# Delta-rule projections: conv taps out of PSUM, all weight remainders on VectorE, first weights by piece

## The reference, cut to what matters

```python
proj = x @ w_in                                   # (256, 1024) @ (1024, 4112)
qkv, z, b, a = jnp.split(proj, [3072, 4096, 4104], axis=-1)
qkv = jax.nn.silu(causal_dwconv(qkv, conv_w))     # 4 taps over time, per channel
q, k, v = jnp.split(qkv, [1024, 2048], axis=-1)   # then 8 heads of 128
q, k = l2norm(q) * 128 ** -0.5, l2norm(k)         # needs sum(t * t) over each head
beta = jax.nn.sigmoid(b)
g = -jnp.exp(a_log) * jax.nn.softplus(a + dt_bias)
... # chunked delta rule, gate with silu(z), w_out, layer norm; then SwiGLU, S5,
... # a mixture of experts, and the second block
```

## Time and profile before

| what | value |
|---|---|
| executions, device time | 1888.09 us median of 3 (1887.85 to 1892.72) |
| profiled execution, first to last instruction (span) | 1885.6 us |
| PE busy | 1613.8 us, 86% |
| DVE busy | 1103.5 us, 59% |
| ACT busy | 700.6 us, 37% |
| POOL busy | 133.3 us, 7% |
| mean granted TensorE clock | 0.914 of full speed |
| stage of the change | first matmul 14.29 us, first z matmul 118.56 us, last z matmul 142.4 us |

### The profile page before, as it was taken

How to read it: one execution, slowest core, us unless ns; L and a number is a source line. 1 busy time by engine, 2 the same in 40 slices (tenths; PEclk the granted TensorE clock), 3 DMA queues, 4 the chain that set the end, 5 groups by cost and what they waited for, 6 DMA issues and landing times.

```text
span 1885.6 us, 25406 instructions
## 1 busy us (share of the span) xinstructions
PE 1613.8 (86%) x9980; PEld 1187.4 (63%) x9980; DVE 1103.5 (59%) x1621; ACT 700.6 (37%) x920; POOL 133.3 (7%) x79
## 2 busy tenths in 40 slices
PE   5896976999774486999999999497699999999995
PEld 5896845898673365888888888386444343443434
DVE  6946646999848755888888887765321212112136
ACT  4443104444320133777677776241112121211222
POOL 5540000000015400000000000000000000000000
PEclk9888987999875596999999999798799999999998
DMA  8321013544530042888888888173299999999950
GB/s 324 135 90 46 3 45 119 192 177 160 231 112 1 0 179 84 306 326 318 305 312 328 332 316 326 40 318 129 110 408 425 422 423 426 421 424 423 423 213 23
DMA packets 36217, 442.82 MB, mean 235 GB/s; under 512 B 5296, under 2 KB 5680, under 8 KB 8624
## 3 DMA queue, kind: packets, MB, share of 16 engines
q1 hardware_dynamic: 33264, 433.58, 58.3%
q10 hardware_dynamic: 2880, 8.23, 1.2%
HBM read 440.74 MB, written 1.05 MB: 234 GB/s over the span
## 4 chain that ended last, share of the span: by engine, by line
PE 54%; DVE 6%; ACT 1%; issue 0%; DVEq 0%; ACTq 0%
PE psum L215 53%; DVE sb_split L1569 1%; ACT sb_split L1564 1%; DVE sb_work L1972 1%; DVE sb_small L290 1%; PE psum L1608 1%; PE psum L1511 0%; PE psum L1858 0%; DVE sb_ring_r L260 0%; DVE sb_xres L1808 0%; DVE sb_work L349 0%; DVEq L211 0%; PE psum L331 0%; DVE sb_work L313 0%; DVE sb_xres L310 0%
## 5 line engine op out<-in xcount | busy, mean ns | idle before, releaser
L215 PE MATMUL psum<-sb_work 64*64 64x64 f32 (+11 forms) x3472 | 444.2, 374 | 96.1 <-POOL sb_work L1428 40.3
L215 PEld LDWEIGHTS psum<-sb_work 128*64 128x64 f32 (+5 forms) x3472 | 254.3, 169 | 266.2 <-issue 187.2
L215 PE MATMUL psum<-sb_split 128*128 128x512 f32 (+1 forms) x1680 | 376.8, 383 | 8.0 <-DVE sb_split L1569 8.0
L215 PEld LDWEIGHTS psum<-sb_split 128*128 128x128 f32 x1680 | 309.7, 189 | 65.6 <-DVE sb_split L1569 11.2
L1569 DVE TENSOR_TENSOR sb_split<-sb_ring,sb_split 128x2048 fp32r<-128x2048 f32 (+1 forms) x144 | 302.5, 2111 | 75.2 <-ACT sb_split L1564 74.3
L1564 ACT ACTIVATE sb_split<-sb_ring 128x2048 fp32r<-128x2048 f32 (+1 forms) x144 | 253.8, 1774 | 116.5 <-PE psum L215 106.7
L215 PE MATMUL psum<-sb_ring,sb_work 128*64 128x512 f32 (+1 forms) x848 | 207.9, 597 | 2.9 <-ACT sb_work L1881 1.3
L215 PEld LDWEIGHTS psum<-sb_ring,sb_work 128*64 128x64 f32 (+1 forms) x848 | 69.2, 143 | 135.9 <-issue 134.8
L215 PE MATMUL psum<-sb_xT_r,sb_ring_r 128*128 128x256 f32 x512 | 146.9, 287 | 0.0
L1970 DVE TENSOR_TENSOR sb_work<-sb_work,psum 128x512 f32<-128x512 f32 x16 | 11.0, 687 | 188.2 <-ACT sb_work L1891 188.2
L1891 ACT ACT_TABLE_LOAD x16 | 20.5, 1283 | 264.2 <-PE psum L215 264.2
(11 more groups left out here) (386 smaller groups left out, 2337.3 us busy)
## 6 DMA issues: line engine op xcount, KB each, us to landing
sb_ring<-moe_wide SPq DMA_DIRECT2D x48, 2048.0 KB, 8.2
sb_ring<-moe_up SPq DMA_DIRECT2D x48, 2048.0 KB, 11.5
sb_work<-moe_down SPq DMA_DIRECT2D x32, 2048.0 KB, 10.5
sb_ring<-w_dense SPq DMA_DIRECT2D x25, 2048.0 KB, 8.0
sb_ring<-moe_last SPq DMA_DIRECT2D x24, 1536.0 KB, 6.7
sb_work<-moe_up SPq DMA_DIRECT2D x16, 2048.0 KB, 13.1
sb_ring<-ffn_wide SPq DMA_DIRECT2D x12, 2048.0 KB, 8.3
sb_ring<-ffn_last SPq DMA_DIRECT2D x6, 1536.0 KB, 6.7
```

Source lines behind the costliest of these rows:

```text
L215: return nc.tensor.matmul(o, lhsT, rhs, start=start, stop=stop, **kw)
```

## The change

- **Conv taps.** ACT no longer copies a piece into `raw`. It writes the last tap (the newest sample times its weight) straight from PSUM into `qkvT` (one ACTIVATE with a scale). DVE adds the other three taps with three scalar_tensor_tensor, each reading the PSUM bank itself, over 255, 254 and 253 columns. They are spread over laps: lap c adds tap 2 of piece c, tap 1 of piece c - 1 and tap 0 of piece c - 2. PE may reuse a bank when `conv_done` says that the last tap was added.
- **Remainders.** All 32 are on DVE, that of piece c + 3 at the head of lap c. POOL has none.
- **Squares.** They move from POOL to ACT, piece c - 3 in lap c, behind the silu of piece c - 2.
- **z.** The fourth z piece's high part (ACT) and remainder (DVE) now stand ahead of the norm's arithmetic, the last four remainders behind the gates'.
- **Loads.** The first six units are laid out piece by piece in memory (a piece is 1024 numbers in a row for each partition), and the first unit is loaded as four transfers of 512 KB, of which the first three have semaphores of their own, so that ACT can begin with the first piece alone.

```diff
@@ gdn: helpers @@
-            w = tile[:, gd_unit(s) % RING, :].rearrange("p (k n) -> p k n", k=DC)
-            return w[:, :, (s % 4) * P:(s % 4 + 1) * P] if s < QKV else ...
+            w = tile[:, gd_unit(s) % RING, (s % 4) * D:(s % 4 + 1) * D]
+            return w.rearrange("p (k n) -> p k n", k=DC if s < QKV else 2)
         def gd_high(act, s):
-            unit_ready(act, gd_unit(s))
+            if s < 3:
+                act.wait_ge(sem(f"piece_loaded{s}"), 16)
+            else:
+                unit_ready(act, gd_unit(s))
@@ gdn_tensor @@
                 if c >= 4:
-                    pe.wait_ge(sem("qkv_evac"), c - 3)
+                    pe.wait_ge(sem("conv_done"), c - 3)
...
-            pe.wait_ge(sem("qkv_evac"), QKV - 3)
+            pe.wait_ge(sem("conv_done"), QKV - 3)
...
-            pe.wait_ge(sem("qkv_evac"), QKV - 2)
+            pe.wait_ge(sem("conv_done"), QKV - 2)
@@ gdn_scalar, for c in range(QKV + 2) @@
                 if c < QKV:
                     gd_high(act, c + 3)
                     act.wait_ge(sem("qkv_ps"), c + 1)
-                    act.activation(raw[:, c, TAPS - 1:], bank[c % 4][:, 0:SEQ], ACT.Copy).then_inc(sem("qkv_evac"), 1)
+                    act.activation(qkvT[:, c, :], bank[c % 4][:, 0:SEQ], ACT.Copy, scale=conv_w[:, c, TAPS - 1:TAPS])\
+                       .then_inc(sem("tap_done"), 1)
                 if c >= 2:
                     act.wait_ge(sem("conv_done"), c - 1)
                     act.activation(qkvT[:, c - 2, :], qkvT[:, c - 2, :], ACT.Silu).then_inc(sem("silu_done"), 1)
+                if 3 <= c < 2 * HEADS + 3:
+                    act.wait_ge(sem("silu_done"), c - 2)
+                    act.activation(sq[...], qkvT[:, c - 3, :], ACT.Square).then_inc(sem("sq_done"), 1)
@@ gdn_vector @@
-            gd_low(v, 2)
-            for c in range(QKV):
-                if c + 3 < QKV and gd_on_vector(c + 3):
-                    gd_low(v, c + 3)
-                v.wait_ge(sem("qkv_evac"), c + 1)
-                ... # tensor_scalar, then three linked scalar_tensor_tensor out of raw
+            for s in range(3):
+                gd_low(v, s)
+            def tap(c, k):
+                late = TAPS - 1 - k
+                acc = qkvT[:, c, late:]
+                return v.scalar_tensor_tensor(acc, bank[c % 4][:, 0:SEQ - late], conv_w[:, c, k:k + 1], acc, ALU.mult, ALU.add)
+            for c in range(QKV + 2):
+                if c < QKV:
+                    gd_low(v, c + 3)
+                    v.wait_ge(sem("tap_done"), c + 1)
+                    tap(c, 2).then_inc(sem("tap2_done"), 1)
+                if 1 <= c <= QKV:
+                    v.wait_ge(sem("tap2_done"), c)
+                    tap(c - 1, 1).then_inc(sem("tap1_done"), 1)
+                if c >= 2:
+                    v.wait_ge(sem("tap1_done"), c - 1)
+                    tap(c - 2, 0).then_inc(sem("conv_done"), 1)
@@ gdn_gpsimd @@
-            g.memset(raw[:, :, 0:TAPS - 1], 0.0).then_inc(sem("pad_done"), 1)
-            for s in range(GD_PIECES):
-                ... # remainders and squares
@@ sync @@
-            for u in range(RING):
+            for i in range(4):
+                sp.dma_start(ring[:, 0, i * D:(i + 1) * D], I["w_dense"][DENSE_AT[U_QKV]][:, i * D:(i + 1) * D])\
+                  .then_inc(sem(f"piece_loaded{i}" if i < 3 else "unit_loaded0"), 16)
+            for u in range(1, RING):
                 dense(u, U_QKV)
```

More of the change, by code:

```diff
@@ L353, in program @@
         cw = Carver(work, 0, WORK)
-        raw = cw(QKV, SEQ + TAPS - 1)
+        cw(QKV, SEQ + TAPS - 1)
         qkvT = cw(QKV, SEQ)
@@ L430, in gd_high, with gd_low @@
             act.activation(gd_buffer(s), gd_piece(ring, s), ACT.Copy).then_inc(sem("gdn_high"), 1)
[L432 to L435, removed]
+        def gd_low(v, s):
+            v.wait_ge(sem("gdn_high"), 1 + s + 1)
+            v.tensor_tensor(gd_piece(ring_r, s), gd_piece(ring, s), gd_buffer(s).bitcast(F32), ALU.subtract)\
+             .then_inc(sem("gdn_low"), 1)
         def gd_split(pe, s):
[L439 to L443, removed]
+            pe.wait_ge(sem("gdn_low"), 1 + s + 1)
         def gdn_tensor(pe):
-            pe.wait_ge(sem("gdn_low_vector"), 1)
             for c in range(QKV):
                 if c >= 4:
-                    pe.wait_ge(sem("qkv_evac"), c - 3)
+                    pe.wait_ge(sem("conv_done"), c - 3)
                 gd_split(pe, c)
@@ L490, in gdn_tensor @@
                         ins.then_inc(sem("z_used"), 1)
-            pe.wait_ge(sem("qkv_evac"), QKV)
+            pe.wait_ge(sem("conv_done"), QKV)
             pe.wait_ge(sem("silu_done"), QKV)
@@ L660, in gdn_scalar @@
                     act.activation(qkvT[:, c - 2, :], qkvT[:, c - 2, :], ACT.Silu).then_inc(sem("silu_done"), 1)
+                if 3 <= c < 2 * HEADS + 3:
+                    act.wait_ge(sem("silu_done"), c - 2)
+                    act.activation(sq[(c - 3) // HEADS][:, (c - 3) % HEADS, :], qkvT[:, c - 3, :], ACT.Square)\
+                       .then_inc(sem("sq_done"), 1)
             act.wait_ge(sem("gates_vector"), 1)
@@ L666, in gdn_scalar @@
             act.activation(sp_a[:, :, :], sp_a[:, :, :], ACT.Ln, bias=1.0).then_inc(sem("gates_act"), 1)
+            gd_high(act, QKV + 3)
             act.wait_ge(sem("gates_vector"), 2)
             act.activation(rn[:, :, :], rn[:, :, :], ACT.Sqrt).then_inc(sem("gates_act"), 1)
-            for s in range(QKV + 3, GD_PIECES):
+            for s in range(QKV + 4, GD_PIECES):
                 gd_high(act, s)
@@ L716, in gdn_vector @@
             v.wait_ge(sem("gdn_high"), 1)
-            v.tensor_tensor(gxl[:, :, :], xT[:, :, :], gxh[:, :, :].bitcast(F32), ALU.subtract).then_inc(sem("gdn_low_vector"), 1)
-            gd_low(v, 2)
-            v.wait_ge(sem("pad_done"), 1)
-            for c in range(QKV):
-                if c + 3 < QKV and gd_on_vector(c + 3):
-                    gd_low(v, c + 3)
-                v.wait_ge(sem("qkv_evac"), c + 1)
[L724 to L730, removed]
+            v.tensor_tensor(gxl[:, :, :], xT[:, :, :], gxh[:, :, :].bitcast(F32), ALU.subtract).then_inc(sem("gdn_low"), 1)
+            for s in range(3):
[6 more added lines that the diff above has]
+                if c < QKV:
+                    gd_low(v, c + 3)
+                    v.wait_ge(sem("tap_done"), c + 1)
[6 more added lines that the diff above has]
+                    tap(c - 2, 0).then_inc(sem("conv_done"), 1)
             v.wait_ge(sem("gates_ps"), 1)
@@ L739, in gdn_vector @@
             dve_link(v, v.tensor_scalar(sp_t[:, :, :], sp_t[:, :, :], 0.0, None, ALU.max))
+            gd_low(v, QKV + 3)
             v.wait_ge(sem("gates_ps"), 2)
@@ L2684, in layouts, with by_piece @@
     glu, w2in = inp["s5_w_glu"][0], inp["w_in_2"][0]
-    units = cols(w_in, 0, 8) + cols(inp["gdn_w_out"][0], 0, 2) + cols(inp["s5_w_in"][0], 0, 2)
+    def by_piece(unit):
+        return unit.reshape(P, DC, 4, P).transpose(0, 2, 1, 3).reshape(P, UNIT)
+    units = [by_piece(u) for u in cols(w_in, 0, 6)] + cols(w_in, 6 * 512, 2) + cols(inp["gdn_w_out"][0], 0, 2) + cols(inp["s5_w_in"][0], 0, 2)
     units += cols(glu, 0) + cols(glu, D) + cols(glu, 512) + cols(glu, D + 512)
```

3 lines of the change are left out of this document (removed).

## The result

| | before | changed |
|---|---|---|
| median, us | 1890.68 (8 runs, 1887.85 to 1893.18) | 1899.04 (8 runs, 1894.04 to 1901.97) |
| ratio | | 1.0047, 95% interval 1.0035 to 1.0058 |
| profiled execution | span 1885.6 | 1898.75, span 1897.0 |
| first matmul | 14.29 | 11.46 |
| one-column matmuls begin | 106.37 | 110.81 |

Slower by 0.47%: 8.4 us between the medians of all runs; 7.6 were forecast, 1895.7 in all. The same views as in the earlier trace rows, now of the changed kernel: the head of its page and its timeline of PE.

The account below looks back on a forecast made before the run. PE was taken as the bound, waiting for remainders on a late DVE. Earlier start, turn-taking laps and slower one-column matmuls put z 7.6 us late: 1885.6 + 7.6 = 1893.2, with 2.5 around it 1895.7; range 1887 to 1905.

Parts of the forecast that it names:

- Start: Before the first matmul: with unit 0 loaded in four parts, PE starts at 11.4 instead of 14.29, 2.9 us earlier.
- Lap: Main loop: ACT and DVE take turns, 4.24 us a lap, 3.79 without the square; PE waits about 1.4.
- End of the loop: After the last lap: one-column matmuls wait for tap 0, begin at 112.7 instead of 106.37; loop 6.3 us late.
- Clock: The 64 one-column matmuls before z: they begin at the lower clock and take 13.5 us, 1.3 more.
- z: The eight z pieces: start at 126.2, 7.6 us late, and run 23.85 us without a wait as before.
- Everything later: Behind z: all is relative to z, so no further shift.
- The short lap: Rival, main loop: lap of 3.86 to 4.14 us, shift 0 to +5.7, middle 1891, no difference; chance 0.26.
- The open circle: Rival, ACT's wait for `conv_done`: circle does not close, PE bounds at 2.83 us a piece, 1869, faster; chance 0.07.
- The swinging clock: Rival, PE in the laps: clock falls, 1905 if in half of the laps, 1914 in all; chance 0.10.
- The rule on PSUM operands: DVE's taps: by the rule none cheaper than 0.51 us with its gap, lap 4.55, total some 6 us higher.

Follow-up runs that it names:

- the reordered kernel: Against the changed kernel, DVE does tap 0 and tap 1 ahead of the remainder and tap 2 in each lap; 1870.04 us, ratio 0.9895 to the kernel before.

## Why the prediction was right, step by step

- **Start.** The first matmul was forecast at 11.4 and came at 11.46; the parts of unit 0 let the second and third high part start at 9.09 and 10.35, both 0.20 us after ACT was free. The pieces behind it came 0.8 us earlier than forecast: the fourth high part is released at 15.99 and not at 16.8. I took 5.39 us for that from the kernel before and said that half of it ran at the lower clock. Its matmuls came one every 0.21 us until 19.1, so it was nearly all of it; in the changed kernel they did so until 14.5 only, and the same step took 4.53 us.
- **Lap.** 4.24 and 3.79 us were forecast, 4.14 and 3.83 measured. Two terms are off by more than 0.05, in opposite directions: from silu to square 0.45 was taken, and 87.29 - 86.97 = 0.32 is measured; from the first of the three taps to the silu 1.22 was taken, and 86.97 - 85.68 = 1.29 is measured. PE's wait a lap, 1.4 forecast, is 1.05.
- **End of the loop.** The one-column matmuls were forecast at 112.7 and began at 110.8. Lap 23 begins 2.2 us earlier than forecast, 0.8 of it for the first pieces and 1.4 for the laps. But the path was not the one forecast. They were to wait for the last tap 0, behind short gate matmuls. In fact the gate matmuls waited for a tap (0.83 us, until 106.85), took 4 us, and the one-column matmuls followed them without a gap, some 0.3 us after that last tap 0. The two paths are nearly as long as each other, so the number held by luck.
- **Clock.** 13.5 us were forecast for the 64 matmuls, 124.46 - 110.81 = 13.65 measured. The reason given was that PE's last piece has ended and PE stands idle before them. The runs don't bear that out: with the silu later and eight banks PE is busy without a gap, and the clock falls all the same soon after the small matmuls begin (gate matmuls from 80.91, one-column ones from 84.39):

```profile
80.00:84.00 4.00, 4.00 (x39) 4.00 (x37) 3.58 (x7) 1.79 (x4) 0.00 (x0) 1.00 0.51 123
84.00:88.00 4.00, 4.00 (x31) 4.00 (x31) 2.61 (x10) 2.91 (x6) 0.00 (x0) 0.81 0.94 401
88.00:92.00 4.00, 4.00 (x20) 4.00 (x20) 0.00 (x0) 3.02 (x5) 0.00 (x0) 0.50 0.01 4
```

- **z.** I let it take 23.85 us as before; it took 25.4, since it stayed 6 us at the lower level and not 3. z's end is 7.4 us late where 7.6 was forecast: two errors of 1.5 to 2 us cancel, which is luck.
- **Everything later.** It was taken as zero. In the profiled executions the span grew by 11.4, so 4 us seem to come behind z. But the profiled execution of before was a short one: it spans 1885.6, and the median of the eight runs less the 1.8 us around a span (1898.75 - 1897.0) is 1888.9. All ten other profiles here, that of the loads alone included, lose 0 to 4 us behind z against it. Between the medians the change costs 8.4, 1.0 more than at z's end, and the runs of one kernel spread by 5 to 8 us. So no loss behind z is shown. (For the same reason the 2.5 us that I took around the span were 0.7 too much; with 1.8 the forecast would read 1895.0.)
- **Rivals.** The short lap, 3.86 to 4.14, isn't refuted by the lap: 4.14 stands on its edge, and z began only 5.9 us late, just what would hardly be told from no change. What put the time clear of it is z's longer stay at the lower clock, which was not foreseen, and what the medians add. The mechanism was right; that the verdict came out as clearly as it did is in part luck. The open circle is what the reordered kernel does, 1870; its price, 1869, was right. The swinging clock is out in the laps: 1.00 in all stretches from 16 to 104 us, with PE busy 5.9 us of 8.
- **The rule on PSUM operands** (Trainium skill, VectorE: DVE Perf Modes, Rules for kernel authors) did not cost anything here: 470 to 476 ns a tap out of PSUM, and 490 for the linked ones in SBUF.

## What to carry to other kernels

When two in-order engines feed each other inside one loop, write down for each wait in which lap its signal is given. A wait on a signal of the same lap closes a circle when the signal stands behind work that itself waits for the waiting engine. The lap is then the sum of the steps that take turns (4.14 us here) and not the work of the busier engine (2.5 us on DVE). Its mark in a profile is that both engines are idle in every lap, each for the other, with moderate busy shares. The two parts of this change that were run alone on the kernel before both gained (the remainders 0.9925, the loads 0.9987), and so did all the rest without the remainders (0.9973); the taps out of PSUM and the squares on ACT were not run alone. The whole lost, and still did with the squares back on GpSimd (1.0021). So ask of a combination what each new instruction is queued in front of.

## What the runs showed of the hardware that was not expected

- GpSimd's 2.40 us remainder held back DVE's taps as long as both of their tensors lay in SBUF (mean 869 ns), and did not when one of the two lay in PSUM: 472 to 481 ns a tap with the same remainders on GpSimd. The Trainium skill (SBUF — State Buffer, SBUF: two separate sides) says that an instruction with two SBUF inputs, or in a two-port mode, and GpSimd take one port pair in turn, whichever comes first for its whole length; these runs agree with it.
- 64 one-column matmuls took 13.65 us in a block with PE busy throughout, and the granted clock stayed at 0.50; in groups of 16 between z's pieces they took 1.84 us each, 7.4 in all, at 0.99 to 1.00.
- A piece of 24 matmuls that starts after a wait releases its readers 3.20 us after its start and the one right behind it 3.08 us after its own, while pieces in a row follow every 2.83 us. A price from start to release is not the price a piece.
